# Setting the steps of a table computation between the products of a dense stage, and giving VectorE the products that GpSimd did

## The reference, cut to what matters

```python
logf = logaddexp(log_lb, log_1m_lb + log_sigmoid(f_pre))
k = -expm1(logf)
```

## Time and profile before

| what | value |
|---|---|
| median of 3 runs | 3055.52 us (3053.34 to 3057.48) |
| the profiled execution's own time | 3057.13 us |
| its span in the trace | 3055.4 us |
| TensorE matmul busy | 2663.2 us, 87% of the span |
| VectorE busy | 1687.2 us, 55% |
| ScalarE busy | 1256.8 us, 41% |
| GpSimd busy | 342.2 us, 11% |

### The profile page before, as it was taken

The page is one execution under the profiler, slowest core; times in us unless marked ns, Lnnn a source line. Parts: engine busy times, 40 slices in busy tenths (PEclk is TensorE's granted clock), DMA queues, the critical chain, the costliest instruction groups (busy, mean ns, idle before and its releaser), DMA issues.

```text
span 3055.4 us, 32379 instructions
## 1 busy us (share of the span) xinstructions
PE 2663.2 (87%) x12877; PEld 2120.5 (69%) x12877; DVE 1687.2 (55%) x1894; ACT 1256.8 (41%) x1416; POOL 342.2 (11%) x411
## 2 busy tenths in 40 slices
PE   4878668967899999867597799999999999999977
PEld 2434554554588878657576698889888988898853
DVE  5476782033222223243833667876687668766862
ACT  2232441011222222134422456765676557655741
POOL 3354761230000000000000000000000000000010
PEclk9989888977999999985698799999999999999999
DMA  7434600200232222224230777987798769976960
GB/s 218 127 116 135 188 1 15 69 0 21 69 97 97 97 88 99 90 110 121 110 131 35 254 247 253 381 290 245 252 373 303 248 243 366 323 248 241 353 240 28
DMA packets 317029, 528.77 MB, mean 173 GB/s; under 512 B 19302, under 2 KB 175562, under 8 KB 314218
## 3 DMA queue, kind: packets, MB, share of 16 engines
q1 hardware_dynamic: 287690, 481.83, 45.9%
q0 software_dynamic: 6000, 26.27, 2.7%
q10 hardware_dynamic: 23184, 18.55, 1.9%
HBM read 497.05 MB, written 47.91 MB: 178 GB/s over the span
## 4 chain that ended last, share of the span: by engine, by line
PE 74%; DVE 8%; ACT 3%; issue 2%; DMA 2%; POOL 0%; SPq 0%; DVEq 0%; ACTq 0%; POOLq 0%
PE psum L1559 23%; PE psum L1232 15%; PE psum L1618 10%; PE psum L1419 5%; PE psum L1141 5%; PE psum L1620 4%; PE psum L1139 2%; PE psum L1476 2%; DVE stages L2410 1%; PE psum L1334 1%; DVE stages_r L2746 1%; PE psum L1495 1%; DVE stages L2379 1%; ACT stages_r L2036 1%; PE psum L1384 1%
## 5 line engine op out<-in xcount | busy, mean ns | idle before, releaser
L2746 DVE TENSOR_TENSOR stages_r<-kept,stages_r 128x2048 fp32r<-128x2048 f32 x336 | 769.0, 2290 | 271.4 <-ACT stages_r L2036 270.7
L1559 PE MATMUL psum<-stages_r 128*128 128x512 f32 x3136 | 746.4, 396 | 21.0 <-DVE stages_r L2801 11.0
L2036 ACT ACTIVATE stages_r<-kept 128x2048 fp32r<-128x2048 f32 x336 | 637.3, 1912 | 263.4 <-PE psum L1559 136.6
L1559 PEld LDWEIGHTS psum<-stages_r 128*128 128x128 f32 x3136 | 589.3, 190 | 148.0 <-DVE stages_r L2746 12.4
L1618 PE MATMUL psum<-stages_r 128*128 128x320 f32 x1792 | 465.8, 346 | 6.3 <-issue 3.2
L1232 PE MATMUL psum<-stages_r 128*128 128x512 f32 x1920 | 443.0, 393 | 17.2 <-DVE stages_r L2525 17.2
L1232 PEld LDWEIGHTS psum<-stages_r 128*128 128x128 f32 x1920 | 365.4, 190 | 94.2 <-issue 17.7
L1620 PE MATMUL psum<-stages_r 128*128 128x160 f32 x1792 | 423.6, 236 | 0.0
L1620 PEld LDWEIGHTS psum<-stages_r 128*128 128x128 f32 x1792 | 343.4, 192 | 2.0
L1618 PEld LDWEIGHTS psum<-stages_r 128*128 128x128 f32 x1792 | 337.7, 188 | 9.0 <-DVE stages_r L2746 3.7
L2525 DVE TENSOR_TENSOR stages_r<-kept,stages_r 128x2048 fp32r<-128x2048 f32 x54 | 123.5, 2292 | 363.6 <-ACT stages_r L1916 363.6
(11 more groups left out here) (373 smaller groups left out, 2686.3 us busy)
## 6 DMA issues: line engine op xcount, KB each, us to landing
kept<-in_moe_w_gu_dram SPq DMA_DIRECT2D x224, 1024.0 KB, 6.4
kept<-in_moe_w_down_dram SPq DMA_DIRECT2D x112, 1024.0 KB, 6.4
kept<-in_ffn_w_gu_dram SPq DMA_DIRECT2D x28, 1024.0 KB, 5.2
kept<-in_ev_w_in_dram SPq DMA_DIRECT2D x16, 1024.0 KB, 6.6
kept<-in_ffn_w_down_dram SPq DMA_DIRECT2D x14, 1024.0 KB, 5.1
s_input_maps<-stages ACTq DMA_DIRECT2D x32, 256.0 KB, 2.5
s_output_maps_by_state<-stages ACTq DMA_DIRECT2D x64, 128.0 KB, 2.2
s_output_maps<-s_output_maps_by_state SPq DMA_DIRECT2D x32, 256.0 KB, 4.7
```

Source lines behind the costliest of these rows:

```text
L1559: m = pe.matmul(out_, a, b, start=start and n == 0, stop=stop and n == len(pairs) - 1, skip_group_check=True)
L2036: act.activation(w_high[n % WSLOTS], unit_tile(n), ACT.Copy).then_inc(s_wh, 1)
L2746: dve.tensor_tensor(w_low[n % WSLOTS], unit_tile(n), w_high[n % WSLOTS], ALU.subtract).then_inc(s_ws, 1)
```

## The change

The table steps are no longer set behind whole slots but in front of single products. Products are counted through all slots (8 to a slot); the first step stands in front of product 52, the fifth of slot 6, and the others follow every 3 or 4 products (3.375 on average). `s5_step(k)` does what the loop behind `dense_block` did. VectorE computes BQ and CQ itself, each just behind the first product of its pair, and s_pq is gone; GpSimd keeps only `add_skip`. On ScalarE a slot's steps are served before its drain, and c_store(k-1) is issued ahead of b_copy(k). `logs_in` is cut in four parts by b, placed behind steps 2 to 5 and 11 to 14, `logs` behind ScalarE's steps 8 and 17, `logs_out` behind steps 10 and 19, and each v copy behind the first step of the next slot.

```diff
-        def step_slot(k):
-            return SLOT0 + k * (SLOTS - SLOT0) // NSTEP
-
-        steps_of = [[k for k in range(NSTEP) if step_slot(k) == n] for n in range(SLOTS)]
+        STEP0 = SLOT0 * KB + KB // 2
+
+        def step_product(k):
+            return STEP0 + k * (SLOTS * KB - STEP0) // NSTEP
+
+        steps_of = [[k for k in range(NSTEP) if step_product(k) // KB == n] for n in range(SLOTS)]
+        step_before = {step_product(k): k for k in range(NSTEP)}
+        LOGS_IN, LOGS_ACT, LOGS_OUT = (2, 11), (8, 17), (10, 19)
...
-            for k in range(NSTEP):
-                g0 = STEP * k
-                if k:
-                    pool.wait_ge(s_bc, 2 * k - 1)
-                pool.tensor_tensor(BQ.rearrange("p g d m c -> p g (d m) c"),
...
-                if k >= 2:
-                    add_skip(k - 2)
+            for k in range(NSTEP - 2):
+                add_skip(k)
...
                     for k in range(4):
+                        s5_step(step_before.get(KB * slot + 4 * kk + k))
                         pair = (w[:, k, b * P:(b + 1) * P], hnT[:, 4 * kk + k, :])
...
+            def s5_step(k):
+
+                if k is None:
+                    return
+                if k % 4 == 1 and k < NSTEP - 4:
+                    c_block(k // 4 + 1)
+                b_step(k)
+                if k:
+                    kernel_step(k - 1)
...
             def logs(d):
-                act.wait_ge(s_lnin, d + 1)
+                act.wait_ge(s_lnin, 4 * d + 4)
...
             for slot in range(SLOTS):
+                for k in steps_of[slot]:
+                    if k % 4 == 1 and k < NSTEP - 4:
+                        c_copies(k // 4 + 1)
+                    if k:
+                        c_store(k - 1)
+                    b_copy(k)
+                    if k:
+                        b_store(k - 1)
+                        kernel_copy(k - 1)
+                    if k >= 2:
+                        kernel_store(k - 2)
+                    for d in range(2):
+                        if k == LOGS_ACT[d]:
+                            logs(d)
                 dense_drain(slot)
...
-            def logs_in(d):
+            def logs_in(d, b):
...
-                chain.link(dve.tensor_scalar(lnb4, lf[d], 1.0 / LN_SPLIT, 1.0, ALU.mult, ALU.min))
+                chain.link(dve.tensor_scalar(lnb4[:, b, :], lf[d][:, b, :], 1.0 / LN_SPLIT, 1.0, ALU.mult, ALU.min))
                 chain.settle()
-                dve.tensor_scalar(lf[d], lf[d], LN_SPLIT, None, ALU.max).then_inc(s_lnin, 1)
+                dve.tensor_scalar(lf[d][:, b, :], lf[d][:, b, :], LN_SPLIT, None, ALU.max).then_inc(s_lnin, 1)
...
+                chain.link(dve.tensor_tensor(BQ.rearrange("p g d m c -> p g (d m) c"),
...
                 chain.settle()
-                dve.wait_ge(s_pq, 2 * k + 1)
                 dve.tensor_tensor(BP[k % 2], BP[k % 2], BQ, ALU.add).then_inc(s_bc, 1)
...
+                chain.link(dve.tensor_tensor(CQ.rearrange("p g d m c -> p (g d) m c"),
...
                 chain.settle()
-                dve.wait_ge(s_pq, 2 * k + 2)
                 dve.tensor_tensor(CP[k % 2], CP[k % 2], CQ, ALU.add).then_inc(s_bc, 1)
...
+            for k in range(NSTEP):
+                powers(k)
+                for d in range(2):
+                    if LOGS_IN[d] <= k < LOGS_IN[d] + 4:
+                        logs_in(d, k - LOGS_IN[d])
+                    if k == LOGS_OUT[d]:
+                        logs_out(d)
+                for b in range(4):
+                    if k == steps_of[4 * gv + b + 1][0]:
+                        v_copy(b)
```

More of the change, by code:

```diff
@@ L322, in build_program @@
         s_cc = sem("s5_c_ready")
-        s_pq = sem("s5_pool_products")
         s_bc = sem("s5_powers_ready")
@@ L1258, in _ @@
                     c_block(0)
[L1259 to L1264, removed]
             kernel_step(NSTEP - 1)
@@ L1780, in c_copies @@
                 if b >= 2:
-                    act.wait_ge(s_pq, 8 * (b - 1))
                     act.wait_ge(s_bc, 8 * (b - 1))
@@ L1832, in _ @@
                     c_copies(0)
[L1833 to L1844, removed]
             b_store(NSTEP - 1)
@@ L2302, in _ @@
                 m.then_inc(s_rc, 1)
-            def logs_in(d):
+            def logs_in(d, b):
                 dve.wait_ge(s_drA, cumA[gidx[("ff", "fb")[d]]])
[L2307 to L2312, removed]
+                dve.tensor_scalar(kT[d][:, b, :], kT[d][:, b, :], hgc[:, 6, b:b + 1], hgc[:, 7, b:b + 1],
+                                  ALU.mult, ALU.add).then_inc(s_k, 1)
+                chain.link(dve.tensor_scalar(lf[d][:, b, :], lf[d][:, b, :], hgc[:, 6, b:b + 1], hgc[:, 5, b:b + 1],
+                                             ALU.mult, ALU.add))
                 chain.settle()
@@ L2334, in powers @@
                                                  [P, STEP, 2 * L5, GC]), ALU.mult))
+                chain.link(dve.tensor_tensor(BQ.rearrange("p g d m c -> p g (d m) c"),
+                                             Bsw[:, g0:g0 + STEP, :].unsqueeze(2).broadcast_to([P, STEP, 2 * L5, GC]),
+                                             WB[:, g0:g0 + STEP].rearrange("p g d m -> p g (d m)").unsqueeze(3).broadcast_to(
+                                                 [P, STEP, 2 * L5, GC]), ALU.mult))
                 chain.settle()
-                dve.wait_ge(s_pq, 2 * k + 1)
                 dve.tensor_tensor(BP[k % 2], BP[k % 2], BQ, ALU.add).then_inc(s_bc, 1)
@@ L2345, in powers @@
                                                  [P, 2 * STEP, M5, GC]), ALU.mult))
+                chain.link(dve.tensor_tensor(CQ.rearrange("p g d m c -> p (g d) m c"),
+                                             Csw[k // 4 % 2][:, gb:gb + STEP].rearrange("p g d c -> p (g d) c").unsqueeze(2).broadcast_to(
+                                                 [P, 2 * STEP, M5, GC]),
+                                             PB[:, g0:g0 + STEP].rearrange("p g d m -> p (g d) m").unsqueeze(3).broadcast_to(
+                                                 [P, 2 * STEP, M5, GC]), ALU.mult))
                 chain.settle()
-                dve.wait_ge(s_pq, 2 * k + 2)
                 dve.tensor_tensor(CP[k % 2], CP[k % 2], CQ, ALU.add).then_inc(s_bc, 1)
@@ L2352, in _, with v_copy @@
             gv = gidx["v"]
[L2353 to L2367, removed]
+            def v_copy(b):
+                dve.wait_ge(s_lam, 16)
+                dve.wait_ge(s_grp, 4 * gv + b + 1)
+                dve.tensor_copy(vtok[:, b, :], psum[:, b, :]).then_inc(s_drD, 1)
+            for k in range(NSTEP):
[8 more added lines that the diff above has]
+                        v_copy(b)
             def scores(n):
```

## The result

The changed kernel takes 3014.1 us (median of 4 runs, 3010.6 to 3014.5) against 3056.5 us for the kernel before in the same comparison. The ratio is 0.9859, 95% interval 0.9842 to 0.9876: 42 us less, where 28.5 were forecast.

A forecast was written before the change was run, and what follows sets the result against it. Waits in a ring between TensorE and VectorE, with no engine full, bounded the stage. From 104.2 us the terms put the last product at 280.1 and the memset at 286 to 287, a 29 us gain: about 3027 us, range 3015 to 3045.

The forecast's parts named there:

- two queues in step: Touched stage: TensorE at 4.61 us a step and VectorE at 4.06 run together; TensorE waits where VectorE has more work.
- waits in a ring: Touched stage: TensorE waits 40.8 us for VectorE, VectorE 39.1 us for TensorE and 23.9 us for c_store's landing.
- Part 1: VectorE does all products: a step takes 4.06 us, a logs_in quarter 2.1 us, VectorE's sum 154 us.
- Part 2: Steps between products on TensorE: 147.4 us of work, plus waits of 12 us for logs_in, 3.5 for logs_out, 4 for logs.
- Part 3: ScalarE's order: c_store issued earlier removes most of the 23.9 us wait; long landings cost 6 us, bounds 0 and 16.
- Part 4: TensorE's clock in the stage: waits mostly 1 to 2 us, so 3 us of loss counted.
- Rival 2: TensorE's clock falls with short stops; at mean clock 0.71 the stage ends 11 us later, 3066 us; chance 0.06.
- Rival 1: Slow c_store landings set the pace: no gain, 3056 us; half that effect, 3042 us, has chance 0.2.
- Rival 4: Looser coupling, logs_in falls into TensorE's 4-product gaps, landings stay short: 14 us more gain, 3013 us; chance 0.05.
- Rival 3: VectorE's 1.5 us sums are not contention: a step costs about 5.7 us, 3056 us; no-gain chance 0.05, shared.

## Why the prediction was right and wrong

The model of two queues in step was right, and the forecast of 28.5 us was too small because of terms that stood in the sum as allowances. The path of the last product, term by term:

| term | forecast, us | measured, us |
|---|---|---|
| step 0 | 104.2 | 105.4 |
| products and steps | 147.4 | 146.4 |
| logs_in | 12 | 9.9 |
| logs_out, and logs and table loads on ScalarE | 3.5 + 4 | 3.0 |
| landings | 6 | 0 |
| clock | 3 | 0 |
| last product ends | 280.1 | 264.7 |
| to the memset | 6 | 7.7 |

The waits measured are what each distance of the transposes has above TensorE's 4.19 or 5.05 us (4.62 with a c_block behind three products), 12.9 us in all: 9.9 before steps 3 to 6 and 12 to 15, 3.0 before steps 11 and 20.

**What bounds the kernel.** Right. The waits in a ring were the cost, and the run that spreads the steps and leaves GpSimd its products is rid of them: TensorE and VectorE wait for each other 11.6 and 2.8 us there, against 40.8 and 39.1.

**Part 1.** The durations were right (4.06 us a step, 0.69 and 0.76 us a sum), and the place in the sum too: VectorE is not the bound of quiet steps. What the text did not say is the consequence, that this half of the change gains little. The run shows it: 3015.0 against 3014.1 us, and 5.8 us in the stage. A quarter of logs_in took 1.83 us, 5.89 - 4.06, not 2.1: the two instructions that were bounded by 0.31 and 0.53 us took 0.43. Over 8 steps that is the 2.1 us by which this term was too large.

**Part 2.** TensorE's sum was off by 1 us, because the last kernel products stand behind the last product and were counted ahead of it. The 4 us for logs on ScalarE were not paid on top of logs_out; what held is the lower bound that the prediction gave for them, "nothing, if it falls into the logs_out wait". The first logs did make TensorE wait, 1.3 us in step 10, in the timeline of the changed kernel:

```profile
154.59 0.60 PE L1197 MATMUL psum<-kept,stages 128*128 128x128 f32 x4
...
155.79 0.54 ACT L1795 ACTIVATE stages<-psum 16x480 f32<-16x480 f32 x1
...
156.39 2.28 DVE L2313 TENSOR_TENSOR stages<-stages 128x2048 f32<-128x2048 f32 x1
...
156.48 1.03 PE L1209 MATMUL psum<-stages 128*16 128x128 f32 x8 [1.29 <-DVE stages L2345]
```

The view names VectorE's sum, but these are the products of step 9, whose map had been ready since 151.67 us. By the kernel's own waits they need ScalarE's kernel_copy of step 8, which came behind logs and two table loads and ended at 156.33; in the run with GpSimd's products the view does name kernel_copy for this wait, 1.3 us too. Then logs_out (line 2313) held up VectorE, and the input map of step 11 was ready at 160.70 us, so without ScalarE's wait step 11, at 160.98, would have come only about 0.2 us sooner. The second logs, behind step 17, cost nothing; the 1.65 us at step 20 are logs_out.

**Part 3.** This is the step that failed, the largest of the terms that did: "It has landed 3.6 us into the step, and VectorE needs it at about 4.1 us", so that a landing of 6 us would come 3 to 4 us late, 6 us in the sum. The need was about right (3.6 to 3.7 us in quiet steps), the issue was put too late. c_store(k-1) does not go out at TensorE's start of step k. It goes out as soon as the output map is complete and ScalarE has finished what stands ahead of it: 2.1 to 3.8 us ahead of TensorE in 16 of the 31 steps, and between 1.5 us ahead and 0.6 us behind in the others, where c_copies, a drain or logs come first. The timeline of the changed kernel around its step 31 (start, length, engine, line; q marks an engine's queue of issues):

```profile
255.44 0.76 DVE L2345 TENSOR_TENSOR stages<-stages 128x576 f32<-128x576 f32 x1
...
257.40 0.90 ACTq L1804 DMA_DIRECT2D s_output_maps_by_state<-stages  x2
...
259.54 0.60 PE L1197 MATMUL psum<-kept,stages 128*128 128x128 f32 x4
```

The map is complete at 256.20, c_store is issued at 257.40, and TensorE's next step is at 259.54. So a landing of 6 us still fits, and the 6 us of the sum were not paid. Long landings did come: the c_stores of steps 4, 14 and 24 took 6.0, 6.3 and 6.0 us. They had gone out 2.3, 2.8 and 3.0 us ahead of TensorE and landed 2.0, 2.3 and 0.6 us before VectorE needed them, the first two in steps in which logs_in held VectorE back. That none of them met a step whose c_store goes out late is luck: in the run with steps that end early one did, and VectorE waited 2.75 us. With the old order, where c_store goes out 1.1 us or more behind TensorE, later than the forecast's picture, the landings cost 10 us. What did not fit was the end, for which no step is left as cover: beside the weight tiles loaded at 259.7 and 264.8 us the last c_store took 6.1 us and the last kernel_store 4.6, and the way to the memset was 1.7 us longer than forecast. With the tiles held it was 4.2 us instead of 7.7.

**Part 4.** The clock cost nothing after step 1: 1.00 from 110 to 240 us, with waits of up to 1.5 us. Rival 2 fell with it, and by the same rows the Trainium skill's warning (TensorE: Matmul & The Clock Gate, "A second HAM failure mode: psum-queue depth-cycling") did not come true here, with 25 breaks of the product runs in those 130 us. A longer wait was followed by the lower clock in the run with steps that end early, 2.4 us; but a wait of 2.6 us at step 20 of the run with one more product was not (transposes of 0.66 us), so no limit can be read from these runs. The 3 us allowed for the clock were not paid.

**The rivals and the range.** Rival 1 was the wrong way round: the landings, which gave it a chance of 0.2, are what the change hides best. Rival 4 came nearest by its time, 3013 us, with a chance of 0.05; that was too little, and by its reasons it is half right and half luck: the coupling was looser, since c_store ran ahead, but landings did not stay short, and logs_in still cost 9.9 of the 12 us. Rival 3 fell with the sums at 758 ns. The allowances for logs, landings and clock made 13 us, all to the slow side, and the range went 12 us below the forecast and 18 above it. By the prediction's own sign, a memset before 275 us, it was wrong: the memset came at 272.41.

## What to carry to other kernels

Where two engines hand work to each other through double buffers and both have other work, set the exchanged steps evenly between it: grouped steps make each wait for the other in turn. Cost the spread order step by step as the slower of the two queues, and ask of every store from when it can be issued, not beside what it stands in the code; an issue that moved two places was worth 10 us here, 4 of them because it no longer stood behind a long piece of other work. Before an engine is relieved of contention, look whether it is the slower queue: taking VectorE's longest sum from 1432 to 758 ns gained at most some 6 us of 42, nearly all in the steps in which VectorE had more to do than TensorE or had just caught up.

## What the runs showed of the hardware

- A 128x576 sum on VectorE took 1432 ns on the mean beside GpSimd's products and 758 without.
- TensorE kept the full clock from 110 to 240 us, with 25 steps (2 to 26) of transposes between products and waits of up to 1.5 us. After a wait of 2.4 us in another run its transposes took 1.11 us instead of 0.60, and after one of 2.6 us in a third they took 0.66.
- Stores of 128 KB that land in 2.0 us in the median took up to 6.2 us (minimum 1.9) with loads of 1 MB tiles in the same stage, and at most 3.2 us from 160 us on with those loads held. The landings of line 1804 in the changed kernel, 98 to 275 us:

```profile
DMA to landing us min/median/max: 1.9/2.0/6.2
```
